# State functions' product in column tiles of 32, sides exchanged and turned back; squares of the norms on VectorE; gates ahead of the state outputs

## What is computed

```python
n = rmsnorm(h, norm1_g);  z = n @ w_in + b_in          # u_s5 512 | conv 2x512 | q 512 | gates 3x1024
mk, mv = rmsnorm(mem) @ w_mem_k, rmsnorm(mem) @ w_mem_v # 256 memory tokens; also returned
# branch A: S5, 32 groups of 16 channels, 64 complex states each
lam_bar = exp(lam * dt);  b_bar = (lam_bar - 1) / lam * b
states = scan(lam_bar, b_bar @ u);  y = Re(C states) + d*u;  zz = gelu(y)
br_s5 = (zz * sigmoid(zz @ glu_w + glu_b)) @ w_s5_proj
# branch B: gated causal convolution (31 taps), layer norm, swish, projection
# branch C: cross attention of q on mk, mv (4 heads of 128), projection
h = h + (g0*br_s5 + g1*br_conv + g2*br_xa) @ w_out
h = h + peer(rmsnorm(h, norm2_g))                       # 8 heads, top 16 of 16384 experts each
y = rmsnorm(h, final_norm_g)
```

## Time and profile before

| | us |
|---|---|
| three runs | 1919.93, 1916.39, 1919.29 |
| median | 1919.29 |
| the profiled execution's own time | 1918.61 |
| its span | 1916.8 |
| PE busy | 1517.8 (79%) |
| DVE busy | 1298.0 (68%) |
| ACT busy | 527.2 (28%) |
| POOL busy | 647.8 (34%) |
| chain that ended last, PE and DMA | 41% and 41% of the span |
| moved by DMA | 675.45 MB, of which the gathers 577.23 MB |

### The profile page before, as it was taken

One profiled execution on the slowest core, in us unless ns is written; L12 is line 12 of the kernel. 1 busy time (PEld: TensorE's weight loads), 2 busy tenths in 40 slices (PEclk: granted clock), 3 DMA queues, 4 the chain that ended last, 5 costly groups with the idle time before them and its releaser, 6 DMA issues.

```text
span 1916.8 us, 22322 instructions
## 1 busy us (share of the span) xinstructions
PE 1517.8 (79%) x7779; PEld 787.3 (41%) x7779; DVE 1298.0 (68%) x3346; ACT 527.2 (28%) x1278; POOL 647.8 (34%) x605
## 2 busy tenths in 40 slices
PE   8999999998879988988888989554556675565567
PEld 7888788786334443443333434111111111111112
DVE  5998665427776766676667667766777767777755
ACT  3111133113333344343223333231122121221212
POOL 0020030004434334444344434434444434444442
PEclk9989999999989999999988999768866888677768
DMA  5453564659999999999999999999999999999997
GB/s 212 144 89 110 176 134 148 195 181 369 420 405 404 418 417 418 417 417 419 419 409 407 420 419 421 406 422 416 411 423 418 400 395 418 421 422 420 420 421 293
DMA packets 112706, 675.45 MB, mean 352 GB/s; under 512 B 12784, under 2 KB 15296, under 8 KB 42576
## 3 DMA queue, kind: packets, MB, share of 16 engines
q0 software_dynamic: 80816, 577.23, 74.0%
q1 hardware_dynamic: 31216, 95.87, 14.1%
q10 hardware_dynamic: 560, 0.92, 0.2%
HBM read 665.79 MB, written 6.21 MB: 351 GB/s over the span
## 4 chain that ended last, share of the span: by engine, by line
PE 41%; DMA 41%; issue 7%; DVE 6%; POOL 2%; ACT 2%; ACTq 0%; POOLq 0%; DVEq 0%
DMA upper<-in_peer_uv,upper 22%; DMA lower<-in_peer_uv,upper 19%; PE pair L1199 12%; PE pair L677 7%; PE pair L688 6%; PE pair L1045 4%; PE pair L791 3%; PE pair L1194 2%; DVE upper L2120 2%; PE pair L991 1%; ACT upper L1598 1%; POOL upper L653 1%; POOL lower L653 1%; DVE lower L2120 1%; PE pair L722 1%
## 5 line engine op out<-in xcount | busy, mean ns | idle before, releaser
L1199 PE MATMUL pair<-upper 64*64 64x512 f32 x2368 | 385.3, 761 | 208.1 <-ACT upper L1598 207.9
L653 POOL DMA_INDIRECT upper<-in_peer_uv,upper x324 | 363.9, 1123 | 508.3 <-PE pair L1199 415.4
L653 POOL DMA_INDIRECT lower<-in_peer_uv,upper x220 | 246.9, 1122 | 462.1 <-PE pair L1199 273.3
L1199 PE MATMUL pair<-lower,upper 64*64 64x512 f32 x1600 | 259.0, 756 | 128.6 <-ACT upper L1598 128.5
L2120 DVE CUSTOM_DVE_ANT_0 upper<-upper 128x1024 f32<-128x1024 f32 x172 | 210.8, 1225 | 122.2 <-DMA upper<-in_peer_uv,upper 122.1
L2120 DVE CUSTOM_DVE_ANT_0 upper<-upper,lower 128x1024 f32<-128x1024 f32 x152 | 186.2, 1225 | 127.5 <-DMA upper<-in_peer_uv,upper 126.7
L1199 PEld LDWEIGHTS pair<-upper 64*64 64x64 f32 x2368 | 91.0, 166 | 407.2 <-ACT upper L1598 273.7
L1598 ACT ACTIVATE upper<-upper 128x64 f32<-128x64 f32 (+2 forms) x543 | 155.4, 338 | 307.5 <-DVE upper L2136 307.3
L1045 PE MATMUL pair<-lower 128*128 128x288 f32 x704 | 214.0, 434 | 3.9 <-ACT upper L1456 3.9
L1406 ACT ACTIVATE upper<-upper 128x4 f32<-128x4 f32 (+1 forms) x141 | 41.9, 297 | 634.8 <-DVE upper L2120 634.7
L2120 DVE CUSTOM_DVE_ANT_0 lower<-lower,upper 128x1024 f32<-128x1024 f32 x116 | 142.1, 1225 | 89.8 <-DMA lower<-in_peer_uv,upper 89.8
(11 more groups left out here) (425 smaller groups left out, 1781.9 us busy)
## 6 DMA issues: line engine op xcount, KB each, us to landing
lower<-in_w_in SPq DMA_DIRECT2D x64, 512.0 KB, 4.8
lower<-in_peer_q SPq DMA_DIRECT2D x28, 512.0 KB, 7.9
lower<-in_proj SPq DMA_DIRECT2D x48, 256.0 KB, 6.6
lower<-in_w_out SPq DMA_DIRECT2D x16, 512.0 KB, 4.8
upper<-in_peer_uv,upper POOLq DMA_INDIRECT x324, 12.8
upper<-in_cache_k SPq DMA_DIRECT2D x8, 512.0 KB, 4.3
upper<-in_cache_v SPq DMA_DIRECT2D x8, 512.0 KB, 4.4
lower<-in_peer_uv,upper POOLq DMA_INDIRECT x220, 13.5
```

The costliest lines, as they stand in the source:

```text
L653: pool.indirect_dma_start(row(g), None, a["peer_uv"], bass.IndirectOffsetOnAxis(ap=idx[:, n % 8, j:j + 1], axis=0)).then_inc(row_in[g % RI ...
L1199: mm = pe.matmul(acc[put, r, :], d[own, 0:64], v[own, h * 512:(h + 1) * 512], start=begun, stop=ended)
```

## The change

- **Head.** The constants are loaded first, x behind k0's weights, `s5_pack` behind v1's. VectorE scales `memT` by the norm's gain alone, and adds the squares over the 8 blocks (7 additions of 256 columns, 7 of 544). TensorE makes k0, k1, k2 from the unscaled `memT`, then one product for each sum of squares (and two of 4 columns, which give mem's sums by rows), then k3 and v. The factor 1/rms is put on keys and values afterwards: on v by ScalarE as it copies (two instructions with a scale per row), on the keys by VectorE (`kT` times `mr`, four products, and the reciprocal of `mr` among them), after it has handed the angles to ScalarE.
- **State functions.** Sides are exchanged: 32 columns of C (16 of the group's own, 16 of the next) are stationary, the 128 of `Epad` move, and four groups go to the four column tiles of 32 ("TT", 64 instructions). ScalarE copies TT (128x1024) to `turned_T`; TensorE does ET0, then turns the copy back with 8 transposes ("T"), then ET1 to ET3. ScalarE's seven transfers stand behind the copy of T as before, but now ET0's copy is ahead of them.
- **Gates.** G4 starts ahead of y0, G5 to G8 stand between y0 and y1, G9 to G11 between y1 and y2. Two matmuls of a gate run ahead of y0 and of y1, 24 are woven in, and six run alone behind y0 and behind y1. Two more gates than before run ahead of y2, two fewer after it.
- **Layer norm.** ScalarE does the four gates of the GLU ahead of the root; VectorE multiplies by them ahead of the reciprocal and its four products.
- **Tail.** Experts 0 to 9 of the last n go in 64x64 form into the block before; only 10 to 15 stay in the block of their own. That block before is added at j = 12 instead of j = 10.

```diff
-JOBS = (["ssm", "ssx"] + [f"k{c}" for c in range(4)] + ["v"]
+JOBS = (["k0", "k1", "k2", "ssx", "ssm", "k3", "v"]
...
-        + ["ag0", "ai0", "ag1", "ai1", "T"] + [f"ET{b}" for b in range(4)]
+        + ["ag0", "ai0", "ag1", "ai1", "TT", "ET0", "T"] + [f"ET{b}" for b in range(1, 4)]
...
-        + [GATES[0], "ss_s"] + GATES[1:4] + ["as0", "y0"] + GATES[4:7] + ["y1"] + GATES[7:10] + ["y2", GATES[10]]
+        + [GATES[0], "ss_s"] + GATES[1:4] + ["as0", GATES[4], "y0"] + GATES[5:9] + ["y1"] + GATES[9:12] + ["y2", GATES[12]]
...
+SPLIT = 10
+def whole(n, j):
+    return EXPERTS[n][0] == TILES or (n == NJ - 1 and j >= SPLIT)
+def block_of(n, j):
+    return BLOCK_OF[n] - int(n == NJ - 1 and j < SPLIT)
...
+            for j in range(3):
+                keys_of_memory(j)
+            ps = begin("ssx")
+            pe.wait_ge(sums_ok, 2)
+            for h in range(2):
+                mm = pe.matmul(ps[:, h, 0:HT], ones, xsq[:, 0, h * HT:(h + 1) * HT], start=True, stop=True)
+            mm.then_inc(full[JOB["ssx"][0]], 1)
...
+            ps = begin("TT")
+            for q in range(G // 4):
+                for i in range(4):
+                    g = 4 * q + i
+                    own = s5p[:, 3 * G + 2 * G * CG + CG * g:3 * G + 2 * G * CG + CG * g + 32]
+                    mm = pe.matmul(ps[32 * i:32 * i + 32, q // 4, P * (q % 4):P * (q % 4) + P], own,
+                                   Epad[:, g, 0:L, :].rearrange("p s i -> p (s i)"), start=True, stop=True)
...
+            turned_functions(0)
+            ps = flat(begin("T"), 1024)
+            emptied(pe, "TT")
+            for q in range(G // 4):
+                mm = pe.transpose(ps[:, P * q:P * q + P], turned_T[:, P * q:P * q + P], ident)
...
+            between = gate_by_gate(4, 13)
+            for i, (lo, hi) in enumerate(PARTS):
+                if i < 2:
+                    alone(between, 2)
+                woven(out_of_states(i, lo, hi), between, 0 if i == 2 else 4)
+                if i < 2:
+                    alone(between, 6)
...
-            glu_gate(0)
-            glu_gate(1)
+            for j in range(HALF):
+                glu_gate(j)
             emptied(act, "lnv")
             act.activation(lrs, lrs, ACT.Sqrt).then_inc(lr_ok, 1)
-            glu_gate(2)
-            glu_gate(3)
...
+            for v, ready in ((msq, msq_ok), (xsq, xsq_ok)):
+                for k in range(1, KD):
+                    dve.wait_ge(ready, k + 1)
+                    link(tt(v[:, 0, :], v[:, 0, :], v[:, k, :], ALU.add))
+                dve.sem_inc(sums_ok, 1)
...
+            link(dve.reciprocal(mr, mr))
+            for j in range(HEADS):
+                emptied(dve, f"k{j}")
+                tt(kT[:, j, :], kT[:, j, :], mr, ALU.mult).then_inc(key_step, 1)
...
+            for j in range(HALF):
+                emptied(dve, f"glu{j}")
+                tt(zg[:, j, :], zg[:, j, :], zz[:, j, :], ALU.mult).then_inc(zg_ok, 1)
             dve.wait_ge(lr_ok, 1)
             link(dve.reciprocal(lrs, lrs))
...
-                    if j == 10 and n and n == BLOCKS[BLOCK_OF[n]][0]:
+                    if j == (12 if n == NJ - 1 else 10) and n and n == BLOCKS[BLOCK_OF[n]][0]:
                         add_block(BLOCK_OF[n] - 1)
```

More of the change, by code:

```diff
@@ L248, in hybrid_step @@
         qT = at(R + 30008, HALF, TOK)
+        turned_T = at(R + 30008, 1024)
         kT = at(R + 32184, HEADS, MEM)
@@ L702, in _, with keys_of_memory @@
             pe.wait_ge(made, 2)
-            ps = begin("ssm")
-            for k in range(KD):
-                pe.wait_ge(msq_ok, k + 1)
-                mm = pe.matmul(ps[:, 0, 0:MEM], ones, msq[:, k, :], start=(k == 0), stop=(k == KD - 1))
-            mm.then_inc(full[0], 1)
-            ps = begin("ssx")
-            for k in range(KD):
-                pe.wait_ge(xsq_ok, k + 1)
-                for h in range(2):
-                    mm = pe.matmul(ps[:, h, 0:HT], ones, xsq[:, k, h * HT:(h + 1) * HT],
-                                   start=(k == 0), stop=(k == KD - 1))
-            mm.then_inc(full[1], 1)
-            for j in range(4):
+            def keys_of_memory(j):
                 w = loaded(f"k{j}")
@@ L723, in _ @@
                 mm.then_inc(full[JOB[f"k{j}"][0]], 1)
+            for j in range(3):
[5 more added lines that the diff above has]
+            mm.then_inc(full[JOB["ssx"][0]], 1)
+            ps = begin("ssm")
+            pe.matmul(ps[:, 0, 0:MEM], ones, msq[:, 0, :], start=True, stop=True)
+            for m in range(2):
+                mm = pe.matmul(ps[:, 1, 4 * m:4 * m + 4], msq[:, 0, m * P:(m + 1) * P], ones[:, 0:4], start=True, stop=True)
+            mm.then_inc(full[JOB["ssm"][0]], 1)
+            keys_of_memory(3)
             ps = begin("v")
@@ L745, in _, with turned_functions @@
             pe.wait_ge(epad_ok, 2)
-            ps = begin("T")
-            for g in range(G):
-                mm = pe.matmul(ps[:, 0, g * CG:(g + 1) * CG], Epad[:, g, 0:L, :].rearrange("p s i -> p (s i)"),
-                               s5C[:, g, :], start=True, stop=True)
-            mm.then_inc(full[JOB["T"][0]], 1)
-            for b in range(4):
+            ps = begin("TT")
[5 more added lines that the diff above has]
+                                   Epad[:, g, 0:L, :].rearrange("p s i -> p (s i)"), start=True, stop=True)
+            mm.then_inc(full[JOB["TT"][0]], 1)
+            def turned_functions(b):
                 ps = flat(begin(f"ET{b}"), 1024).rearrange("p (g n) -> p g n", g=8)
@@ L756, in _ @@
                 mm.then_inc(full[JOB[f"ET{b}"][0]], 1)
+            turned_functions(0)
[3 more added lines that the diff above has]
+                mm = pe.transpose(ps[:, P * q:P * q + P], turned_T[:, P * q:P * q + P], ident)
+            mm.then_inc(full[JOB["T"][0]], 1)
+            for b in range(1, 4):
+                turned_functions(b)
             weighted("ag2", nT)
@@ L880, in woven, with alone @@
                         next(large, None)
-                for _ in large:
-                    pass
+            def alone(large, count):
+                for _ in range(count):
+                    next(large)
             scores(0)
@@ L905, in _ @@
             mm.then_inc(full[JOB["ss_p"][0]], 1)
-            gates(16, 18)
-            between = gate_by_gate(18, 21)
+            gates(17, 19)
+            between = gate_by_gate(19, 22)
             for _ in sample_values():
@@ L915, in _ @@
             pe.transpose(ps[:, 0, 0:P], Ps[:, 0:P], ident).then_inc(full[JOB["ss_x"][0]], 1)
-            gates(21, 24)
+            gates(22, 24)
             pe.wait_ge(chunks_ok, HALF - 1)
@@ L1342, in _ @@
                            accum_out=asum[:, 0:1]).then_inc(exp_ok, 1)
-            gates(14, 16)
+            gates(16, 17)
             ps = filled(act, "ss_p")
@@ L1642, in _ @@
                 stt(nT[:, k, :], nT[:, k, :], c("g1", k), xr, ALU.mult, ALU.mult).then_inc(n_ok, 1)
+            dve.wait_ge(rms_ok, 2)
+            dve.reciprocal(mcol, mcol).then_inc(key_step, 1)
             W = 9 * G
@@ L1946, in _ @@
                 stt(cact[:, j, :], cact[:, j, :], c("lg", j), lrs, ALU.mult, ALU.mult).then_inc(lnx_ok, 1)
-            for j in range(HALF):
-                emptied(dve, f"glu{j}")
-                tt(zg[:, j, :], zg[:, j, :], zz[:, j, :], ALU.mult).then_inc(zg_ok, 1)
             added_up = 0
```

119 lines of the change are left out of this document (66 added, 53 removed).

## The result

| | before | after |
|---|---|---|
| median of the runs, us | 1918.44 (4 runs, 1916.39 to 1919.93) | 1886.90 (4 runs, 1886.43 to 1888.51) |
| ratio | | 0.9838, 95% interval 0.9821 to 0.9855 |
| profiled execution, span, us | 1916.8 | 1884.6 |
| first gather, us | 434.14 | 405.41 |
| from the first gather to the last addition of the experts, us | 1475.2 | 1471.7 |

The account below looks back on a forecast made before the run. TensorE's time ahead of the first gather, then a byte-bound gather stream, was taken to bound the kernel. 7.4 + 9.4 + 9.9 + 2.7 + 1.8 = 31.2 us; 1918.6 - 31.2 = 1887.4 us, range 1881 to 1897.

Parts of the forecast that it names:

- One for one: Stream of expert-row gathers: bound by its bytes, so time won ahead of the first gather moves the end equally.
- D: As the stream starts, late weights and gathers collide, three to seven more slow stretches: 1896 to 1908 us; chance 0.06.
- E: Early stream: TensorE meets a lower clock and frees ring rows late, holding gathers: 1932 us; chance 0.03.
- Rival A: State functions: TensorE stays at 1.2 GHz, or the column tiles don't overlap: 1890 to 1895 us; chance 0.13.
- Late next: VectorE's scan, next to be late, ends at 194.4 us; TensorE wants it at 197.0, slack 2.6 us.
- Rival B: VectorE is late with the scan, or U with its loads: 1889.5 to 1893 us; chance 0.17.
- Rival C: Gates: the wait on y0 moves to G8 and the clock still falls: 4.3 us, 1891.7 us; chance 0.07.
- just in time: One gate fewer ahead of ScalarE's Gelu: it just finds its operand, priced at nothing, 1 us if cover fails.

Follow-up runs that it names:

- e1: The changed kernel with its old head put back (TensorE adds the squares, memT scaled ahead of the keys): 1895.57 us, ratio 0.9882.
- e2: The changed kernel with the old state functions (products with 16 moving columns, then 32 transposes): 1899.62 us, ratio 0.9903.
- e3: The changed kernel with the gates in their old order (G4 to G6 between y0 and y1, none alone): 1895.76 us, ratio 0.9879.
- e4: The changed kernel with the layer norm's old order (root ahead of the third gate, reciprocal and products ahead of the gates): 1891.55 us, ratio 0.9863.
- e5: The changed kernel with the old tail (last n all in 128x128 form, block before added at j = 10): 1889.96 us, ratio 0.9847.
- e6: The changed kernel with the turned product's same 64 instructions issued one column tile after another: 1892.30 us, ratio 0.9858.
- e8: The changed kernel with three more multiplications on VectorE at the start of the scan: 1889.90 us, ratio 0.9843.
- e7: The changed kernel with the six gate matmuls behind y0 and behind y1 moved ahead of them: 1895.71 us, ratio 0.9876.
- e10: The changed kernel with the old state functions (Epad stationary), but 32 columns of C moving instead of 16: 1898.52 us, ratio 0.9894.
- e11: The changed kernel with 14 of the 16 instructions of the last key k3 left out: 1888.25 us, ratio 0.9840.

## Why the prediction was right

The time, 1886.90 us, lies 0.5 from the forecast of 1887.4. That it is so near is luck in part: after's four runs span 2.1 us and the ratio's interval is 3 us to either side, and the parts below miss by up to 0.9 us in both directions. What stands is that each step can be held against its row. By the part undone alone, and the tail by its column:

| part | predicted | measured |
|---|---|---|
| head | 7.4 | 7.1 (e1) |
| state functions | 9.4 | 10.3 (e2); 9.7 as 16.5 - 6.8 |
| gates | 9.9 | 9.4 (e3) |
| layer norm | 2.7 | 2.3 (e4) |
| tail | 1.8 | 1.8 (e5) |
| sum | 31.2 | 30.9 |

- **What bounds the kernel.** One for one holds: with the first gather anywhere from 402.3 to 415.8 us, the rest took 1472.8 to 1474.1 us in every kernel with the new tail but after itself. With the old tail it took 1475.2 us from 434.1 (before) and 1475.0 from 405.2 (e5). So nothing is lost as the stream starts sooner, and D and E are out for this range of starts.
- **Head.** TensorE started at 7.76 us (7.4 predicted), k0 took 5.52 us at the slow start (6.0 predicted), the wait for k1's weights was 0.93 us instead of 0.5, and k2 ended at 21.39 instead of 20.9. The sums were ready at 19.4, nT at 33.1, Epad at 97.7. The steps are right to half a microsecond, and the half microsecond is when the transfers land.
- **State functions.** 1.93 us instead of 2.3 for the product, 6.8 instead of 7.1 in all. Taking the samples' values as the nearest shape was right: e6 shows that their price holds only because neighbouring instructions use different column tiles, which both have. Rival A is out. The trace of after does not show the clock falling in transposes: it is 1.00 in the slices from 98 to 106 us, which hold 40 of them, and in e2 it rose from 0.50 to 0.80 between 110 and 114 us, while TensorE ran nothing else. So the Trainium skill's sentence that the full clock doesn't engage for transposes ("TensorE: Matmul & The Clock Gate", Part 4) does not hold for the float32 transposes of this kernel. The same page's Part 3 gives 2.38 times for three column tiles of 512 columns; the 3.1 times of e6 for four tiles of 128 columns is a like gain.
- **Late next.** The scan ended at 195.3 (194.4 predicted) with 1.6 us of slack where 2.6 had been worked out; by e8 it is up to 2.1. The scan began 1.1 us later than worked out (149.3 for 148.2): Epad came 0.6 later than the 97.1 forecast, and from there to the scan VectorE took 51.6 us in after, 51.1 in e4, e5 and e7. Rival B did not happen, but it was nearer than the gain of 31 us lets one think: more than 1.6 to 2.1 us of further work on VectorE ahead of the scan would have moved the first gather. The loads of U came in time.
- **Gates.** Rival C is out: from the first of L820's 18 instructions behind y0 (215.39) to the next instruction (219.57) it took 4.2 us, where they take 3.9 without a wait (0.216 each), so the wait at G8 was some 0.3 us, as predicted (0.3 to 0.5), and the clock stayed. The cover for ScalarE's Gelu, which I had put "just in time" at 1 us if it fails, did fail (2.02 us of waiting for ybuf's transfer), and cost TensorE nothing, since TensorE takes what the Gelu makes 23 us after it is done (at 276 us, for glu0 at 299). The step that priced this at up to 1 us was too cautious: it had not asked how long ScalarE's result lies before TensorE takes it.
- **Layer norm.** 1.56 and 0.95 us of waiting for 1.8 and 1.0 predicted. In e4 eight instructions ran slow (3.66 us, 1.7 lost) where 1.9 had been put for sixteen. By e4's rows the terms are 3.56 - 1.56 + 1.7 - 0.95 = 2.7 us, as predicted, but the first gather moved by 2.3. 0.2 of the difference lies ahead of the layer norm (TensorE ran out of work at 314.45 us in e4 and at 314.64 in after). The other 0.2 is that the wait at the fifth product cost more than its idle time: that product starts 2.8 us behind the fourth (321.49 to 324.32) where 1.7 is usual, 1.1 us for 0.95, and the sixth follows 0.1 later than usual.
- **Tail.** 1.8 us, as a mean over eleven profiles, and by the wait of the last addition (e5). After's own profile alone would have said 3.5.

## What to carry over

Where a small product keeps loading a wide stationary side, exchange the sides, and let neighbouring instructions go to different column tiles: both steps are needed, and the order of issue alone is worth 4 of the 10 us here. Where two outputs must share a buffer, put enough independent work directly behind the first (here six matmuls, 2.6 us, for an emptying of 2.9) and not ahead of it: a wait of 2.5 us cost 4.1 with what follows it. Shortening one engine's path is worth what the next engine's slack allows, so work out that slack before the second round: here it was 1.4 us at Epad and 1.6 at the scan, and the next 3.1 us taken off TensorE gave 0.5, since VectorE's chain also grew by 1.05 us. And read such a slack from several executions: the one at the scan was 1.6 to 2.1 us.

## What the runs showed that was not expected

- The clock fell with 32 moving columns as with 16 (e10), both with PEld busy in all of each slice; it stayed at 1.00 with 128 moving columns, also where the tiles ran one by one with PEld just as busy (e6).
- A gap alone does not tell what the clock does. Behind 2.6 us of waiting it fell to 0.50 in e7, behind 2.64 us ahead of the turned product in e11 it stayed at 1.00. The two differ in what TensorE did before (72-column products with gates between them, against products of 272 columns) and after. Which of it decides was not tried.
- Small operations of VectorE (128x32, 0.18 us) took 0.4 to 0.63 us while GpSimd issued transfers. It was seen, not varied; moving those four transfers would tell.
- From one execution to the next the stretch from the first gather to the last addition takes the same time within 1.4 us, and in a single one it was 1.1 us shorter than in all the others. A part worth 2 us behind the first gather cannot be read from one profile.
